# Attention on one Trainium2 core: exponentials multiplied with the values before they are divided by their sums

## The reference

```python
# 16 heads of 64, 4 groups of keys and values; T = 512 tokens, f32
q = q * 64 ** -0.5
gates = sigmoid(gates)                      # (token, 3 branches, head)
p_c = masked_softmax(q @ k_cmp - slope * distance)    # 31 compressed keys
p_s = masked_softmax(q @ k_sel - slope * distance)    # causal
p_w = masked_softmax(q @ k_win - slope * distance)    # causal
o = gates[0] * (p_c @ v_cmp) + gates[1] * (p_s @ v_sel) + gates[2] * (p_w @ v_win)
return (o * silu(z)) @ w_out
```

## Time and profile before

| | us |
|---|---|
| runs | 1391.63, 1395.32, 1396.14 (median 1395.32) |
| span of the profiled execution | 1387.1 |
| PE busy | 1296.2 (93%) |
| DVE busy | 821.5 (59%) |
| POOL busy | 818.7 (59%) |
| ACT busy | 407.6 (29%) |
| DMA | 137.94 MB, mean 99 GB/s |

### The profile page before, as it was taken

The page is one execution under the profiler, slowest core; times in us unless marked ns, Lnnn a source line. Parts: engine busy times, 40 slices in busy tenths (PEclk is TensorE's granted clock), DMA queues, the critical chain, the costliest instruction groups (busy, mean ns, idle before and its releaser), DMA issues.

```text
span 1387.1 us, 22871 instructions
## 1 busy us (share of the span) xinstructions
PE 1296.2 (93%) x8136; PEld 1030.0 (74%) x8136; DVE 821.5 (59%) x1336; ACT 407.6 (29%) x782; POOL 818.7 (59%) x1041
## 2 busy tenths in 40 slices
PE   6999789899999999999998999899999998999986
PEld 4778688678887788888786888555557786878874
DVE  6968896569879411399407426378773559632223
ACT  4265100425310033211210021577773201231111
POOL 7777201487899877899776817300004874467862
PEclk9999899999999999999999999999999999999998
DMA  5222100143224533245493212100005359423321
GB/s 194 78 76 76 39 3 2 46 126 108 91 89 161 159 120 94 91 136 172 110 342 106 91 31 84 39 2 1 1 2 203 100 145 280 168 69 99 93 81 68
DMA packets 86479, 137.94 MB, mean 99 GB/s; under 512 B 16512, under 2 KB 34432, under 8 KB 85376
## 3 DMA queue, kind: packets, MB, share of 16 engines
q1 hardware_dynamic: 48384, 88.10, 20.6%
q10 hardware_dynamic: 38016, 48.71, 10.9%
HBM read 119.02 MB, written 20.91 MB: 101 GB/s over the span
## 4 chain that ended last, share of the span: by engine, by line
PE 75%; DVE 11%; issue 4%; POOL 3%; ACTq 3%; ACT 2%; DMA 2%; POOLq 0%; DVEq 0%
PE ps L372 18%; PE ps L374 18%; PE ps L373 18%; PE ps L706 3%; PE ps L717 3%; PE ps L729 3%; ACTq L1052 2%; POOL small L1285 1%; DVE acc L1359 1%; PE ps L542 1%; PE ps L610 1%; PE ps L655 1%; PE ps L786 1%; DVE bigB L1514 1%; DVE bigB L1892 1%
## 5 line engine op out<-in xcount | busy, mean ns | idle before, releaser
L1288 POOL TENSOR_TENSOR wl<-raw,wh 128x512 fp32r<-128x512 f32 x336 | 497.5, 1481 | 26.9
L1285 POOL TENSOR_TENSOR small<-small 1x1 f32<-1x1 f32 x336 | 118.2, 352 | 335.4 <-PE ps L374 330.1
L372 PE MATMUL ps<-uH,wh 128*128 128x512 f32 x672 | 266.8, 397 | 18.1 <-DVE uL L1349 11.1
L373 PE MATMUL ps<-uL,wh 128*128 128x512 f32 x672 | 263.0, 391 | 0.0
L374 PE MATMUL ps<-uH,wl 128*128 128x512 f32 x672 | 262.8, 391 | 0.0
L1286 POOL CAST wh<-raw 128x512 fp32r<-128x512 f32 x336 | 203.8, 606 | 0.0
L372 PEld LDWEIGHTS ps<-uH,wh 128*128 128x128 f32 x672 | 127.0, 189 | 48.1 <-issue 16.2
L373 PEld LDWEIGHTS ps<-uL,wh 128*128 128x128 f32 x672 | 127.2, 189 | 27.3 <-issue 1.4
L374 PEld LDWEIGHTS ps<-uH,wl 128*128 128x128 f32 x672 | 127.0, 189 | 26.4
L372 PE MATMUL ps<-ffH,wh 128*128 128x512 f32 x256 | 101.3, 396 | 4.4 <-POOL wl L1288 4.3
L373 PE MATMUL ps<-ffL,wh 128*128 128x512 f32 x256 | 99.8, 390 | 0.0
(11 more groups left out here) (380 smaller groups left out, 2442.8 us busy)
## 6 DMA issues: line engine op xcount, KB each, us to landing
raw<-wstream SPq DMA_DIRECT2D x336, 256.0 KB, 2.6
b_powers_scratch<-bigB ACTq DMA_DIRECT2D x4, 1024.0 KB, 4.7
c_powers_scratch<-bigB ACTq DMA_DIRECT2D x8, 512.0 KB, 4.1
lags_scratch<-lag_rows_scratch ACTq DMA_DIRECT2D x8, 512.0 KB, 9.5
bigB<-b_powers_scratch ACTq DMA_DIRECT2D x4, 1024.0 KB, 8.7
bigB<-lags_scratch ACTq DMA_DIRECT2D x4, 1024.0 KB, 8.5
bigB<-c_powers_scratch ACTq DMA_DIRECT2D x4, 1024.0 KB, 11.1
hT<-x ACTq DMA_DIRECT2D x4, 512.0 KB, 7.0
```

Of the source, the lines that this page charges most:

```text
L372: pe.matmul(out, lh, rh, start=first, stop=False)
L373: pe.matmul(out, lh, rl, start=False, stop=False)
L1285: pool.tensor_tensor(small[0:1, 569 + j:570 + j], zero_ap[0:1], zero_ap[0:1], ALU.add)
L1288: pool.tensor_tensor(wl[:, j, :], raw[:, j, :], wh[:, j, :].bitcast(f32), ALU.subtract).then_inc(half_split, 1)
```

## The change

Probabilities are no longer divided by their sums and weighted before they are turned. `turn` now waits for the exponential itself. The order of units becomes t, b, qt, so that four units, one branch of a head pair, form a group g (16 in all), with their sums in `asum`. For each group DVE computes the reciprocal of the 4 x 2 sums times the gates (`gates_by_sums`, in `rsum`), PE spreads them with `spread`: eight products of `rsum`, broadcast over 64 columns as weights, with the identity, into bank 5. DVE multiplies bank 5 with the activated z (`rz`), and then the group's value sums, which each branch now has in a bank of its own (6 or 7), with `rz` (`finish`). The results of the branches are added in SBUF. The compressed branch becomes one section of 512 columns for each pair (`cmp_values`) in bank 6, which DVE multiplies with z into `mixT` (`cmp_branch`). For narrow units (qt 0 and 1) `turn` puts both halves in bank 4, and only qt 2 and 3 use bank 5; the transposes of qt 2 wait until `rz` of the group before has been read. Elsewhere some semaphores are merged into one with higher counts.

```diff
-        asum = small[:, 544:550].rearrange("p (u b) -> p u b", b=2)
-        UNITS = [(t, qt, b) for t in range(KT) for qt in range(TT) for b in range(2)]
+        asum, rsum = (small[:, at:at + 16].rearrange("p (g t a) -> p g t a", g=2, a=2) for at in (576, 592))
+        rz, branch = bigA[:, 14336:14848], bigA[:, 14848:15360]
+        UNITS = [(t, qt, b) for t in range(KT) for b in range(2) for qt in range(TT)]
...
             def turn(u):
                 t, qt, b = UNITS[u]
-                pe.wait_ge(at_p, u + 1)
+                pe.wait_ge(at_e, u + 1)
                 if u >= 1:
                     pe.wait_ge(at_ev, u)
+                if qt == 2 and u >= 4:
+                    pe.wait_ge(at_g, 2 * (u // 4) - 1)
                 for half in range(2):
                     for kt in range(qt + 1):
-                        i = pe.transpose(ps[:, 4 + half, kt * 128:(kt + 1) * 128], prob[:, u % 3, half, kt * 128:(kt + 1) * 128], ident)
+                        at = (half * 512 if qt >= 2 else half * 256) + kt * 128
+                        i = pe.transpose(ps[:, 4 + at // 512, at % 512:at % 512 + 128],
+                                         prob[:, u % 3, half, kt * 128:(kt + 1) * 128], ident)
                 i.then_inc(at_t, 1)
+            def spread(g):
+                pe.wait_ge(at_r, g + 1)
+                pe.wait_ge(at_ev, 4 * g + 4)
+                for qt in range(TT):
+                    for half in range(2):
+                        i = pe.matmul(ps[64 * half:64 * half + 64, 5, qt * 128:(qt + 1) * 128],
+                                      rsum[:, g % 2, qt, half:half + 1].to_broadcast([128, DH]), ident, start=True, stop=True)
+                i.then_inc(at_rt, 1)
...
+            def cmp_values(t):
+                if t:
+                    pe.wait_ge(at_g, 2 * (2 * t - 1))
+                for half in range(2):
+                    g = t // 4 * 2 + half
+                    i = pe.matmul(ps[64 * half:64 * half + 64, 6, :], vcmp[:, g * DH:(g + 1) * DH], pcT[:, half * 8 + t, :],
+                                  start=True, stop=True)
+                i.then_inc(at_c, 1)
             for n in range(len(UNITS) + 3):
                 if n < len(UNITS):
                     scores(n)
                 if 2 <= n <= len(UNITS) + 1:
                     turn(n - 2)
+                if n >= 6 and n % 4 == 2:
+                    spread(n // 4 - 1)
                 if n >= 3:
                     values(n - 3)
+                if n < len(UNITS) and n % 8 == 0:
+                    cmp_values(n // 8)
...
-            def weigh(u):
...
+            def gates_by_sums(g):
+                t, b = g // 2, g % 2
+                dve.wait_ge(at_e, 4 * g + 4)
+                own(dve.reciprocal(rsum[:, g % 2], asum[:, g % 2]))
+                dve.tensor_tensor(rsum[:, g % 2], rsum[:, g % 2], gate[:, :, 1 + b, t::KT], ALU.mult).then_inc(at_r, 1)
+            def cmp_branch(t):
+                dve.wait_ge(at_c, t + 1)
+                dve.tensor_tensor(mixT[:, t, :], ps[:, 6, :], zsT[:, t, :], ALU.mult).then_inc(at_cr, 1)
+                dve.wait_ge(at_cr, t + 1)
+            def finish(g):
+                t, b = g // 2, g % 2
+                dve.wait_ge(at_rt, g + 1)
+                dve.tensor_tensor(rz, ps[:, 5, :], zsT[:, t, :], ALU.mult).then_inc(at_g, 1)
+                dve.wait_ge(at_g, 2 * g + 1)
+                dve.wait_ge(at_v, 4 * g + 4)
+                dst = branch if b else xs[:, t % 2, :]
+                dve.tensor_tensor(dst, ps[:, 6 + b, :], rz, ALU.mult).then_inc(at_g, 1)
+                dve.wait_ge(at_g, 2 * g + 2)
+                if b:
+                    dve.tensor_tensor(xs[:, t % 2, :], xs[:, t % 2, :], branch, ALU.add).then_inc(x_full, 1)
+                else:
+                    own(dve.tensor_tensor(xs[:, t % 2, :], xs[:, t % 2, :], mixT[:, t, :], ALU.add))
-            for n in range(len(UNITS) + 1):
+            for n in range(len(UNITS) + 4):
                 if n < len(UNITS):
                     shift(n)
-                if n >= 1:
-                    weigh(n - 1)
-                if n >= 12 and n % 8 == 4:
-                    finish(n // 8 - 1)
-                if n >= 15 and n % 8 == 7:
+                if n < len(UNITS) and n % 8 == 0:
+                    cmp_branch(n // 8)
+                if n >= 4 and n % 4 == 0:
+                    gates_by_sums(n // 4 - 1)
+                if n >= 7 and n % 4 == 3:
+                    finish(n // 4 - 1)
+                if n >= 14 and n % 8 == 6:
                     finish_rest(n // 8 - 1)
-            finish(KT - 1)
             finish_rest(KT - 1)
```

More of the change, by code:

```diff
@@ L260, in build @@
         s_wgate, wgate_split = sem("w_gate_loaded"), sem("w_gate_split")
-        g_mm, g_scaled, g_rows, g_out = sem("gate_product"), sem("gate_scaled"), sem("gate_rows"), sem("gates_ready")
+        g_mm, g_scaled, g_out = sem("rms_columns_and_gate_product"), sem("gate_scaled"), sem("rms_columns_and_gates_ready")
         blk_done, cmp_h, cmp_act, cmp_mm, cmp_out = (sem(f"compress_{n}") for n in
@@ L267, in build @@
         ds_ready = sem("slopes_ready")
-        at_qk, at_s, at_e, at_p, at_t, at_ev, at_v, at_o = (sem(f"att_{n}") for n in
-            ("scores", "scores_read", "exp", "probs", "transposed", "probsT", "value", "out"))
+        at_qk, at_s, at_e, at_t, at_ev, at_v, at_o = (sem(f"att_{n}") for n in
+            ("scores", "scores_read", "exp", "transposed", "probsT", "value", "out"))
+        at_r, at_rt, at_g, at_c, at_cr = (sem(f"att_{n}") for n in
+            ("gates_by_sums", "gates_by_sums_turned", "group_read", "cmp_value", "cmp_value_read"))
         s_bc = sem("ssm_bc_loaded")
@@ L301, in build @@
         rms_sum, r_ready, rms_norm, rms_out = sem("rms_sum"), sem("rms_roots"), sem("block_output"), sem("rms_out")
-        eps_mixed, rcol_mm, rcol_out = sem("rms_both_sums"), sem("rms_columns"), sem("rms_columns_out")
-        w_both = sem("both_norm_weights")
+        both_ready = sem("both_norm_weights_and_sums")
         conv_tap, z_gated, sz_scaled, sz_gated, zs_gated = (sem(n) for n in
@@ L633, in _ @@
                 i = pe.matmul(ps[:, 4, tt:tt + 1], rms[0:1, tt * 128:(tt + 1) * 128], ones[0:1, 0:1], start=True, stop=True)
-            i.then_inc(rcol_mm, 1)
+            i.then_inc(g_mm, 1)
             pe.wait_ge(tile_evicted, TILE0["val"])
@@ L649, in _ @@
             pe.wait_ge(s_w1, 32)
-            pe.wait_ge(rcol_out, 1)
+            pe.wait_ge(g_out, 1)
             for x in range(2):
@@ L658, in _ @@
                 i.then_inc(cmp_h, 1)
-            pe.wait_ge(g_rows, 1)
+            pe.wait_ge(g_out, 2)
             for tt in range(TT):
@@ L670, in _ @@
             pe.wait_ge(cmp_act, 2)
-            pe.wait_ge(g_out, 1)
+            pe.wait_ge(g_out, 3)
             for g in range(NG):
@@ L722, in values @@
                 pe.wait_ge(at_ev, u + 1)
-                if t >= 2 and qt == 0 and b == 0:
-                    pe.wait_ge(at_o, t - 1)
-                o = [ps[64 * half:64 * half + 64, 6 + t % 2, qt * 128:(qt + 1) * 128] for half in range(2)]
+                if qt == 0:
+                    if t >= 1:
+                        pe.wait_ge(at_g, 2 * (2 * t + b - 1))
+                    if b == 0:
+                        pe.wait_ge(at_cr, t + 1)
                 for kt in range(qt + 1):
@@ L728, in values @@
                         g = t // 4 * 2 + half
[L729 to L735, removed]
-                i.then_inc(at_v, 1)
+                        i = pe.matmul(ps[64 * half:64 * half + 64, 6 + b, qt * 128:(qt + 1) * 128],
+                                      vtok[:, kt, b * 256 + g * DH:b * 256 + (g + 1) * DH],
+                                      probT[:, u % 3, half, kt * 128:(kt + 1) * 128], start=kt == 0, stop=kt == qt)
+                i.then_inc(at_v, 1)
+            def cmp_values(t):
[6 more added lines that the diff above has]
+                i.then_inc(at_c, 1)
             for n in range(len(UNITS) + 3):
@@ L1078, in _ @@
             act.wait_ge(zero_stored, 16)
-            act.wait_ge(w_both, 1)
+            act.wait_ge(both_ready, 1)
             for k in range(KT):
@@ L1090, in _ @@
             act.wait_ge(rms_sum, 3)
-            act.wait_ge(eps_mixed, 1)
+            act.wait_ge(both_ready, 2)
             act.activation(acc[:, 0, :], ps[:, 4, :], ACT.Ln, scale=1.0 / D, bias=eps_ap)
@@ L1110, in _ @@
                     act.dma_start(swapped[64 * par:64 * par + 64, n, :], nsT[64 - 64 * par:128 - 64 * par, 8 + n, :]).then_inc(swapped_in, 16)
-            act.wait_ge(rcol_mm, 1)
-            act.activation(rcol, ps[:, 4, 0:TT], ACT.Copy).then_inc(rcol_out, 1)
+            act.wait_ge(g_mm, 1)
+            act.activation(rcol, ps[:, 4, 0:TT], ACT.Copy).then_inc(g_out, 1)
             act.wait_ge(half_used, 2 * SLOT0["val"] + KT)
-            act.wait_ge(rcol_out, 1)
+            act.wait_ge(g_out, 1)
             for tt in range(TT):
@@ L1117, in _ @@
```

(19 more changed lines are left out.)

1 line of the change is left out of this document (added).

## The result

The changed kernel takes 1402.48 us (median; 1401.87 to 1404.17), beside 1393.47 (1390.65 to 1396.14) for the kernel before in the same sessions. The ratio is 1.0065, 95% interval 1.0045 to 1.0085: slower, by 9.0 us. The profiled execution spans 1400.2 us.

The account below looks back on a forecast made before the run. PE was taken as the bound, busy 93% of the span. Fill 14.6, cycles and compressed sections 149.7 and tail 12.05 us moved the projection's start by +9.1: 1395.3 + 9.1 = 1404.4 us, range 1397 to 1412.

Parts of the forecast that it names:

- PE is the limit of the stage: From first score product to output projection, PE's section times add up; 18.4 us a head pair before the change.
- Removing the weighting is worth its waits: Weighting in front of the turned probabilities: removal gains at most PE's 12.9 us of waits, 1.6 a pair.
- fill: Stage start to second four-tile scores: 12.6 us of PE sections, 0.8 eviction waits, 1.2 for lowered clock.
- V4: PE's values section of four 128-key tiles, following spread; same array shape, so no gap between them was charged.
- B: Rival: spread's two halves run one after the other, +0.86 us in each of 16 groups, 1418; chance 8%.
- C: Rival: a gap also between spread and V4, +2.6 us, 1407; inside the forecast's 80%, no chance of its own.
- T3: PE's three-tile transposes of query tile 2, writing bank 5; predicted to idle PE 0.84 us, 15 times, for rz.
- A: Rival: the bank-5 wait for rz doesn't bind, 12.6 us less, 1391.8; chance 12%, whole or in part.
- The evictions are hidden by 0.2 to 0.4 us: Evictions of three- and four-tile transposes finish before PE needs them, with 0.2 to 0.4 us to spare.
- Pace: Time per head pair in the stage: two group cycles of 10.19 us plus 1.01 for the compressed section, 21.39.
- tail: From the last four-tile scores to the first product of the output projection: 12.05 us.
- E: Rival: the stage's start runs at full clock, 1.2 us less, 1403; inside the forecast's 80%, no chance of its own.

Follow-up runs that it names:

- the last but one kernel: Changed kernel with rz ahead of the shift, plus the shift releasing ACT's exponential half by half: 1389.37 us, ratio to the kernel before 0.9978.

## Why the prediction was right

It was 1404.4 and the time 1402.5; against the sessions' medians it was +9.1 and +9.0. The mechanism is the one that was forecast. That the two differences agree to 0.1 us is luck: errors of over 1 us cancel in the sum, and the clock differs from one execution to the next. Point by point:

- *PE is the limit of the stage, and its sections can be added up.* Right: 18.52 us a pair without the weighting against 18.4, and 19.91 in the last but one kernel against 19.7.
- *Removing the weighting is worth its waits.* Right: with nothing put in its place it gave 12.7 us behind the fill, a little more than the 11.5 that the waits view lists there (12.9 in the whole stage, put as the most). The whole stage became 15.4 us shorter; the 2.7 us in the fill are in part the clock of 0.57 there, up to 1.7, which only the trace of the kernel before has.
- *Spread costs 0.86 us a group, all of it on the path, and has no gap before V4.* Right: spread with V4 was put at 1.88 and takes 1.89 from its start to that of the next section; twice the products cost 14.0 us of stage, against 13.8. The rival with halves one after the other (B) and the one with another gap (C) are out. The gap goes with the change of shape, as the earlier trace rows had it: the move of spread shows 0.16 us. The Trainium skill states it so ("TensorEngine Tiling (Array Packing)", Key Properties: a change of the tiling mode drains the engine), and the trace agrees, with 0.16 us for the additional change.
- *T3 waits for rz, 0.84 us, 15 times.* Right: 0.82 us and 12.8 in all. Moving rz removed it, doubling rz lengthened it by its own time. The rival without it (A) isn't what the kernel does. It is what the moved rz does, but for the eviction of T3, which A had left hidden: 1393.9 instead of 1391.8.
- *The evictions are hidden by 0.2 to 0.4 us.* Right in the changed kernel (1.0 us in all, in the fill and at the end), because T3 is late. It was no reserve: once T3 wasn't late, the eviction behind the four-tile exponential came next.
- *Pace.* 21.39 us a pair, measured 21.54 (948.56 to 970.10 between the three-tile transposes of every second group). Step mis-sized: from rz's start to PE's 0.75 was put, and it takes 0.83 (969.27 to 970.10), so 0.08 twice a pair. I had taken the way from DVE to PE as 0.07 us; it is 0.14 behind rz.
- *Fill, pace and tail.* Three errors that cancel, so that the stage was put at 176.3 us and took 176.5. The fill was put at 13.4 us and 1.2 for the lowered clock of the earlier trace rows; it took 13.3 (888.81 to 902.14), as here the clock didn't fall, which is the rival (E):

```profile
892.00:896.00 4.00, 3.39 (x24) 1.92 (x26) 2.68 (x12) 4.00 (x13) 0.00 (x0) 1.00 0.00 0
```

It didn't fall there in any trace but the one of the kernel before, so nothing ties the 1.2 us to a start full of waits. From the second four-tile scores to the last it was put at 149.7 us and took 150.8 (902.14 to 1052.95), by the mis-sized pace. The tail was put at 12.05 and took 12.37. Then the clock fell right behind the stage, where PE had been idle for 3.0 us, against 2.2 in the earlier trace rows:

```profile
1064.00:1068.00 4.00, 2.68 (x7) 2.13 (x8) 0.69 (x1) 0.54 (x1) 0.00 (x0) 0.73 0.31 70
1068.00:1072.00 4.00, 4.00 (x16) 3.24 (x15) 0.00 (x0) 0.00 (x0) 1.91 (x3) 0.84 1.01 356
```

That is up to 1.7 us (4 x 0.27 + 4 x 0.16) outside the stage, which the sum didn't have. The longer tail isn't shown to be the reason: without the weighting the idle time was the 2.18 us of the kernel before, and the clock fell all the same (0.67 in the first 4 us of the projection, where the kernel before has 1.00); with rz later it was 3.49 us and the clock stayed at 1.00. Why it falls in one execution and not in another is open.

The pieces nearly close. The stage lasts 151.7 us without the weighting; 14.0 for spread, less 8 x 0.44 = 3.5 for one compressed section (1.00 us, from 971.47 to 972.47, where PE runs it) instead of four of 0.36, give 162.2. The kernel that has neither serial wait, with exponentials released half by half, took 164.2, and the two waits then cost 12.3 (176.5 less 164.2). Of the 2.0 us between 162.2 and 164.2, 1.4 lie in the tail: from the last four-tile transposes to the projection it is 7.2 us (1058.12 to 1065.32 in the changed kernel), where the kernel before needed 5.8. The rest is open. The new order of the units and the merged semaphores were not tried by themselves; the latter act ahead of the stage, and in the scatter of the stage's starts no effect of theirs can be seen.

## What to carry to other kernels

Moving elementwise work from DVE onto PE's path pays only if PE waits for DVE by more than the new products take: here some 13 us of waits were exchanged for 14 us of products, and a new wait of 12.8 us came with them. When a scheme reuses a PSUM bank, look where its reader stands in the reading engine's program: the reader here stood behind an operation that waits for later work of PE, and moving it ahead gave back 8.5 us. Behind each wait removed, work out at once which one is next; here it was 0.5 us behind, on a third engine, and releasing one half at a time removed it.

## What was not expected of the hardware

- With a regular idle time of PE of 1.6 us a group, its granted clock came down several times within the stage (means of 0.66 to 0.71 over 10 us), and the delay cost 21 us instead of 11. With 0.8 us a group the mean clock of the stage was 1.00.
- The last idle time before a stretch doesn't tell its clock: behind the stage the first 4 us of the projection had 1.00 after an idle time of 2.18 us and after one of 3.49, but 0.67 after another of 2.18 and 0.57 after one of 2.97.
- Eight f32r products with weights of 128 columns and 128 moving columns take 0.11 us each, no less than sixteen passes in f32 with weights of 64 columns, two side by side, at 0.055 each.
- PE's transposes start 0.14 us behind the printed end of the DVE tensor_tensor that releases them (rz ends at 969.96, they start at 970.10).
